# First mixer's attention on one core: the diagonals of factors are made by GpSimd, not by ScalarE

## What is computed

```python
logits = einsum('bqhd,bqkd->bhqk', qb, k_sel) * scale      # 8 sparse heads, keys chosen by top_k
prob = softmax(where(valid, logits, -inf))
o_lat = einsum('bhqk,bqkl->bqhl', prob, v_sel)             # then lifted by w_uv
...
s = einsum('bqhcd,bshcd->cbhqs', qb, k) * scale            # 4 differential heads, two maps each
prob = softmax(where(mask, s, -inf))
a = prob[0] - lam * prob[1]
o = rms_norm(einsum('bhqs,bshe->bqhe', a, v), subln_g)
```

## Time and profile before

| | |
|---|---|
| median of three runs | 3105.97 us (3105.34 to 3105.99) |
| profiled execution, its own time | 3105.71 us |
| its span | 3104.4 us |
| mean granted TensorE clock | 0.992 of full speed |
| busy: TensorE, VectorE, ScalarE, GpSimd | 3009.7, 1306.5, 1196.8, 1108.4 us |
| chain that ended last: TensorE, VectorE, ScalarE | 85%, 10%, 2% of the span |
| diagonals (L2300) | 64 ScalarE instructions, 526.3 to 653.3 us, median 401 ns (386 ns where the input is the gate) |
| slab splits (L466) | 449 GpSimd instructions, 1093.9 us |

### The profile page before, as it was taken

One profiled execution on the slowest core, in us unless ns is written; L12 is line 12 of the kernel. 1 busy time (PEld: TensorE's weight loads), 2 busy tenths in 40 slices (PEclk: granted clock), 3 DMA queues, 4 the chain that ended last, 5 costly groups with the idle time before them and its releaser, 6 DMA issues.

```text
span 3104.4 us, 36005 instructions
## 1 busy us (share of the span) xinstructions
PE 3009.7 (97%) x14256; PEld 2457.1 (79%) x14256; DVE 1306.5 (42%) x2322; ACT 1196.8 (39%) x2099; POOL 1108.4 (36%) x465
## 2 busy tenths in 40 slices
PE   8999999899999999999999999998999999999998
PEld 6888777778888878888768888887767878888787
DVE  5311288624121271121796232156734243357532
ACT  3322365754232352222434233245333343267522
POOL 4444433014444444444103444443423442320143
PEclk9999999999999999999999999999999999999999
DMA  4322332013333233333212333333312334410132
GB/s 150 95 95 95 91 113 89 1 34 98 99 95 96 95 91 99 95 97 101 92 61 95 102 95 95 96 96 102 123 61 76 100 116 143 146 48 2 35 96 74
DMA packets 78187, 278.27 MB, mean 90 GB/s; under 512 B 8599, under 2 KB 9495, under 8 KB 77636
## 3 DMA queue, kind: packets, MB, share of 16 engines
q1 hardware_dynamic: 78020, 275.96, 27.8%
HBM read 273.78 MB, written 6.08 MB: 90 GB/s over the span
## 4 chain that ended last, share of the span: by engine, by line
PE 85%; DVE 10%; ACT 2%; issue 1%; POOL 0%; DMA 0%; ACTq 0%; SPq 0%; DVEq 0%; POOLq 0%
PE ps L491 25%; PE ps L493 25%; PE ps L492 25%; DVE arena L2690 2%; PE ps L1810 1%; DVE arena L2072 1%; PE ps L3405 1%; PE ps L1795 1%; PE ps L2740 1%; PE ps L2223 1%; PE ps L2237 1%; DVE w_lo L476 1%; PE ps L3198 1%; DVE arena L2156 1%; PE ps L1578 0%
## 5 line engine op out<-in xcount | busy, mean ns | idle before, releaser
L466 POOL TENSOR_TENSOR w_lo<-ring,w_hi 128x1024 fp32r<-128x1024 f32 x449 | 1093.9, 2438 | 1863.5 <-ACT w_hi L443 1863.5
L491 PE MATMUL ps<-x_hi,w_hi 128*128 128x512 f32 x2168 | 857.3, 395 | 29.6 <-DVE x_lo L877 13.1
L493 PE MATMUL ps<-x_hi,w_lo 128*128 128x512 f32 x2168 | 847.5, 391 | 0.0
L492 PE MATMUL ps<-x_lo,w_hi 128*128 128x512 f32 x2168 | 847.1, 391 | 0.0
L443 ACT CAST w_hi<-ring 128x1024 fp32r<-128x1024 f32 x473 | 494.0, 1046 | 720.6 <-PE ps L493 713.2
L491 PEld LDWEIGHTS ps<-x_hi,w_hi 128*128 128x128 f32 x2168 | 409.3, 189 | 121.6 <-issue 22.5
L492 PEld LDWEIGHTS ps<-x_lo,w_hi 128*128 128x128 f32 x2168 | 409.3, 189 | 88.3 <-issue 4.1
L493 PEld LDWEIGHTS ps<-x_hi,w_lo 128*128 128x128 f32 x2168 | 408.9, 189 | 86.4
L491 PE MATMUL ps<-r_hi,w_hi 128*128 128x512 f32 x1120 | 436.1, 389 | 0.4 <-DVE r_lo L1146 0.4
L492 PE MATMUL ps<-r_lo,w_hi 128*128 128x512 f32 x1120 | 435.7, 389 | 0.0
L493 PE MATMUL ps<-r_hi,w_lo 128*128 128x512 f32 x1120 | 435.7, 389 | 0.0
(11 more groups left out here) (313 smaller groups left out, 3341.4 us busy)
## 6 DMA issues: line engine op xcount, KB each, us to landing
ring<-in_stream SPq DMA_DIRECT2D x473, 512.0 KB, 3.5
arena<-in_cmp_w SPq DMA_DIRECT2D x16, 512.0 KB, 3.6
frev_copies<-frev SPq DMA_DIRECT2D x16, 240.0 KB
arena<-frev_copies SPq DMA_DIRECT2D x1, 3072.0 KB, 13.1
h<-in_x SPq DMA_DIRECT2D x4, 512.0 KB, 7.6
out<-arena SPq DMA_DIRECT2D x4, 512.0 KB
arena<-in_p SPq DMA_DIRECT2D x2, 512.0 KB
arena<-in_mem SPq DMA_DIRECT2D x1, 1024.0 KB
```

Source lines behind the costliest of these rows:

```text
L466: self.nc.gpsimd.tensor_tensor(self.w_lo[:, n % SPLIT, :], self.ring[:, n % RING, :], self.w_hi[:, n % SPLIT, :].bitcast(F32), ALU.subtrac ...
L491: nc.tensor.matmul(out, a[0], b[0], start=start, stop=False)
L492: nc.tensor.matmul(out, a[0], b[1], start=False, stop=False)
L493: return nc.tensor.matmul(out, a[1], b[0], start=False, stop=stop)
```

## The change

`scale` is taken out of ScalarE's block and its call out of ScalarE's order. A block for GpSimd does the same for all 32 pairs in a row: the same two waits, the same two 128 x 128 results, the same signal. The instruction is a `tensor_scalar` with a multiplication by a factor per partition in place of an activation with Copy and a scale. Buffers, waits of the others and TensorE's order are as they were.

```diff
+        @block.gpsimd
+        def _(pool):
+            for p in range(n):
+                pool.wait_ge(factor.handle, factor.at(p + 1))
+                if p >= 2:
+                    pool.wait_ge(turned.handle, turned.at(p - 1))
+                for j in range(2):
+                    ins = nc.gpsimd.tensor_scalar(dg[p % 2][:, j, :], gate if pairs[p].joined and j else k.c("ident"),
+                                                  inv[:, p % 3, j:j + 1], None, ALU.mult)
+                ins.then_inc(diag.handle, 1)
+
         @block.scalar
         def _(act):
-            def scale(p):
-                act.wait_ge(factor.handle, factor.at(p + 1))
-                if p >= 2:
-                    act.wait_ge(turned.handle, turned.at(p - 1))
-                for j in range(2):
-                    ins = nc.scalar.activation(dg[p % 2][:, j, :], gate if pairs[p].joined and j else k.c("ident"), ACT.Copy, scale=inv[:, p % 3, j:j + 1])
-                ins.then_inc(diag.handle, 1)
-
...
                 if 1 <= it < n + 1:
                     copy(it - 1)
-                if it < n:
-                    scale(it)
                 subln.act(act, it - norm_at)
```

## The result

The changed kernel takes 3111.05 us, the median of 14 runs (3108.65 to 3112.45); the kernel before took 3105.98 us in 14 runs beside it (3102.65 to 3107.82). The ratio is 1.0017, 95% interval 1.0010 to 1.0024: 5.1 us slower, where 2.8 us faster was forecast. It lies outside the range and on the other side; 7.9 us are to be explained.

A forecast was written before the change was run, and what follows sets the result against it. No engine is full: a loop round the engines bounds the stage of 32 pairs. Gains of 0.9 us (reciprocal to turn) and 1.9 us (SubNorm steps on ScalarE) make 2.8, so 3103.2 us; range 3099.5 to 3108.5.

The forecast's parts named there:

- Part 1: Path from VectorE's reciprocal through the diagonals to TensorE's turn: GpSimd's 0.32 us per instruction gives 0.9 us gained.
- 18 us for each us of price: Each 0.1 us more per GpSimd instruction costs 0.2 us at nine places, 1.8 us.
- the nine places: Waits on the chain between reciprocal and turn: five short pairs, three long pairs and the first pairs, once.
- The whole sum: Both gains in the stage of the 32 pairs: 0.9 + 1.9 = 2.8 us gained.
- The hand-overs: Signals around GpSimd's pair of diagonals: 0.08 us from VectorE's reciprocal to GpSimd, 0.05 us from GpSimd to TensorE.
- Part 2: SubNorm steps queued behind diagonals on ScalarE start earlier: squares gain 1.0 us, the root's table load 0.9, together 1.9.
- Part 3: Queues and cover: the first diagonal isn't behind GpSimd's last split, SyncE's order is untouched, ScalarE's other freed time gains nothing.
- Slow GpSimd pair: Rival: GpSimd's pair becomes the new wait between reciprocal and turn; at 0.9 us an instruction 8.3 us slower; 8%.
- break-even: GpSimd time per instruction, 0.475 us, from which the slow GpSimd pair decides.
- VectorE and GpSimd hold each other up: Rival: at five short pairs GpSimd waits for VectorE's two bias instructions, losing 2.9 us, so 3106.1; 12%.
- Clock: Rival: earlier column sums spare TensorE's clock fall at 611 to 615 us, gaining 1.7 us more; 12%.
- a low clock at other places: Sign that the forecast is wrong: TensorE's low clock appears elsewhere in the changed kernel's profile; no size given.

The follow-up runs named there:

- the two profiles of equal clock: Changed kernel plus 12 unused TensorE products ahead of the fourth pair's turn (3109.46 us), beside the second profile of the unaltered kernel before (own time 3103.02 us).
- the product form: Changed kernel, but GpSimd multiplies the identity by a broadcast factor as second tensor instead of a factor per partition: 3104.54 us against 3106.87, ratio 0.9995.
- the two pairs alone: Kernel before, with GpSimd making only the diagonals of the two pairs beside the SubNorm's squares and root: 3104.72 us against 3105.54, ratio 0.9996.
- the row of prices: Kernel before, plus GpSimd instructions of several forms and widths that nobody waits for and whose result isn't used: 3106.74 us, one run.

## Why the prediction was wrong

**Part 1, the price of GpSimd's instruction: this step failed.** "One input lies between no input and two" gave 0.32 us, at most 0.42. A two-input operation was sized rightly by it (the product took 0.40 in the kernel), but a multiplication by a factor per partition isn't between a fill and a product: at 0.60 us it is dearer than both, by its 2.5 ns a column and 282 ns fixed. By the prediction's own 18 us for each us of price, 0.28 us are 5.1 us, of the 7.9 that are missing. With 0.60 put in, part 1 would be 4.2 us lost; the stretches up to the fourth turn and from the fifth to the 23rd lost 0.9 + 4.1 = 5.0. So the nine places were 0.8 us too few, mostly by the first pair; a small miss beside the price. The whole sum with 0.60 says 2.3 us slower, and the two profiles of equal clock differ by 3.0. With 0.40 it says 1.3 us faster, and the product form measured 0.9995, 1.6 us faster, within an interval of 2.8 us to either side. The hand-overs were right: 0.09 for 0.08, 0.06 for 0.05.

**Part 2: right.** The squares win 1.1 us and the root 0.9 to 1.1, for 1.0 and 0.9. The time of the two pairs alone can't confirm it: 1.2 us in the runs (0.9996, an interval from 1.6 us slower to 4.0 faster); both of its profiles have slow sums, 5.23 and 5.04 us for 3.70, which take back most of the gain.

**Part 3: right.** The first diagonal starts at 525.01 us, behind its reciprocal (which ends at 524.91); GpSimd's last split had begun at 521.46 and taken 2.35 us.

**The rivals.** *Slow GpSimd pair*, at 8%, is what happened: the 0.60 measured lies between its break-even of 0.475 us and the 0.9 that it priced. It was right in mechanism, and given too small a chance, because "no row shows a fixed part over 0.13 us" was held against it when none of the rows was this operation. *VectorE and GpSimd hold each other up*: refuted. The instruction takes the same in the changed kernel and in the row of prices, its durations beside the bias and the search are nearly one value, and VectorE's busy time in the stage is 87.8 us in both kernels:

```profile
L2300 POOL TENSOR_SCALAR arena<-cst,arena x48: 599/602/696, 525.0 to 656.6; 128x128 f32<-128x128 f32 x48
```

(least, median, most, in ns). By the rule of the Trainium skill (SBUF — State Buffer, Who interferes with whom) these VectorE instructions leave GpSimd free; the trace agrees: of 48 instructions the longest took 696 ns, the median 602. *Clock*: the prediction priced it only as a gain, and named a low clock at other places as a sign of being wrong without a price. A later diagonal makes TensorE idle longer, and at the fourth turn that brought one more fall, 1.7 us of lack, worth 1.6 us from the fourth turn to the fifth. That term was missing altogether. It is a consequence of the price: with the 0.40 us form there is no fall.

5.1 for the price, 0.8 for the places and 1.6 for the clock, less 0.1 for part 2, are 7.4 of 7.9 us. The last 0.5 is within the interval of the measured ratio (2.2 us to either side), and the clock at the sums, which differs between executions, could make it too. The count of diagonals on the chain, 15 for ten, is no measure of this: the product form has them on it 20 times and isn't slower than the kernel before.

## What to carry to other kernels

Price an instruction by a row of that very operation on that very engine, at that size; where the profile has none, an operation with more inputs is no upper bound, and the range must reach past the rows. Moving work to an idle engine pays only if the way through it is no longer: here one instruction on each of two engines at once was better than two on either. Where TensorE already idles near a fall of its clock, ask of a later release not only what it delays but whether it adds a fall. And where the whole time hides a term of 1 us, cut the trace at the starts of one repeated step: those stretches came out the same to 0.04 us where whole executions differed by 2.7.

## What the runs showed that was not expected

- On GpSimd a multiplication of 128x128 float32 by a factor per partition takes 602 ns, by a constant 528, as a product with a broadcast factor 401, and a cast 291 (the constant and the cast into fp32r).
- TensorE's clock at one place differs between executions of one kernel: the sums took 3.70 us in two profiles of the kernel before and 6.31 in the third. Single profiles can't be compared to the us without the clock beside them.
- The length of one wait doesn't decide a fall: at the fourth turn TensorE idled for 1.87 us with VectorE's diagonals and the clock fell, and for 2.00 us in one profile of the kernel before and 2.18 with the product form and it did not.
